# Scan stage of a one-layer backbone: round order of a pass, and 256 KB transfers issued one after another

## The chip, the cores and the metric

The kernel runs on one core of one Trainium2 chip. The metric is device time in microseconds of one execution; lower is better.

## The reference

One layer on 2048 latent and 256 context tokens of width 1024: modulated norm, an input projection, two mixers, a merge, and an expert-choice mixture of experts. The scan stage computes the recurrent cores of both mixers. For RWKV-7, in two directions and 8 heads of 64:

```python
def rwkv7_scan(inputs, s0):
    def step(s, inp):
        r_t, w_t, k_t, v_t, kk_t, a_t = inp
        sa = jnp.einsum('bhvk,bhk->bhv', s, -kk_t)
        s = (s * w_t[:, :, None, :] + sa[..., None] * (kk_t * a_t)[:, :, None, :]
             + v_t[..., None] * k_t[:, :, None, :])
        return s, jnp.einsum('bhvk,bhk->bhv', s, r_t)
```

and for the RG-LRU a causal convolution of 4 taps, two gates, `bt = sqrt(-expm1(2 log_a)) * (ig * xc)`, and the scan `h = a h + bt` over time, 512 channels, two directions.

## The kernel before, in words

The program is a sequence of stages written with explicit semaphores; each engine's order is the order of the code, so an instruction that waits holds up everything behind it on its engine. `scan` (L2111) is one of the stages. It makes 18 passes (`LAST` is 17), each over 256 tokens of a direction pair, cut into four chunks of 64. `U` counts two units of four heads.

A call `body(a, c)` interleaves two passes: `a` is solved (the triangular system of each chunk), while `c`, the pass before, is carried through its four chunks of state. The solve of `a` has five rounds (`begin`, `joint`), the **begin phase**, and then five doubling levels:

- round 0: L and its transpose Lt from `aq` and `ob`, 64x64 matmuls into banks 2 and 3 of each unit; ACT copies L, DVE masks Lt into T (T0);
- rounds 1 and 2 (`joint`): products B and K of both units side by side, `ob` with `aq` and `over` with `over`, 64x128 matmuls. Unit 0 does B first and unit 1 K first. DVE evicts each with eight masked multiplies (W0 and Lb from B, La and Lk from K);
- round 3: transposes tB and V; round 4: the transpose tK; ACT copies all three;
- level m: F = H x W (`forward`), ACT copies F; W and T products (`square`), DVE adds them to W and T. POOL makes the masked H of each level from L, and adds the unit matrix to T0 and W0 (`start_solve`).

Between the rounds and levels, at the places of the table `STATE_AT` (X, Z, S with Y for chunks 0 to 3), PE does the state products of pass `c`, and ACT, DVE and POOL the steps of the RG-LRU: at X the gates (ACT) and the series (DVE), at Z the roots and squares (ACT, with two table loads in chunk 0) and the taps (DVE), at S the window (ACT) and, in chunks 0 and 2, two recurrences (DVE). Every engine follows this same order.

Operands come from HBM. `ob` and `over` have one buffer a unit and `aq` has two, since the states read it a pass later. SP waits for tK of both units and then issues the next pass's `ob` and `over` (`reload`, L2225 to L2227); after Y3 and Sb3 of both units come `aq` of the pass after next (`reload_own`, L2223) and eight stores of y (`store`, L2246). It waits for no landing. POOL meanwhile sums `w_mod` slices of 512 KB each (`load`, `add`, L2752 to L2764), ACT loads the convolution's rows `raw` of 1 MB (`load_raw`, L2460). Helper lines: L2273 is every 64x64 matmul of the solve, L2288 every joint one, L2607 every eviction of B and K.

## Time and profile before

| | |
|---|---|
| median of 3 runs | 4309.09 us (4306.44 to 4311.71) |
| the profiled execution | 4309.31 us, its span 4307.5 us |
| mean granted clock of TensorE | 0.932 of full speed |
| PE busy | 3596.5 us, 83% of the span |
| DVE, ACT, POOL busy | 2432.9, 1889.2, 1258.8 us |
| moved by DMA | 610.18 MB, mean 142 GB/s |

How to read it: busy times overlap across engines, and a busy share of a whole span is an average over stages with different limits. Times in rows are microseconds from the first instruction. A clock of 1.00 is 2.4 GHz, 0.50 is 1.2 GHz. A wait put down to "issue" is one for which the profile shows no semaphore's release just before.

### The profile page before, as it was taken

To read this page: it belongs to the slowest core of one execution; us is meant where nothing else is said; L and a number is where in the kernel's file an instruction comes from. 1 tells how busy PE (TensorE), PEld (TensorE's weight loads), DVE (VectorE), ACT (ScalarE), POOL (GpSimd) and SP (SyncE) were. 2 spreads that over 40 slices of the span, in tenths; PEclk is the share of its full clock that TensorE was granted. 3 is DMA by queue.
4 is the path that set the end of the run, shared out by engine and by line. 5 is a ranking of instruction groups with operands and counts; after the bars stand their busy time and mean duration, and the time that the engine had idled before them with its cause. 6 is when DMAs were issued, how large, how long until landed. Compare 5 with 4: busy or idle time off the path is not lost. (4 is left out here: it accounts for less than half of the span.)

```text
span 4307.5 us, 117683 instructions
## 1 busy us (share of the span) xinstructions
PE 3596.5 (83%) x50061; PEld 3199.9 (74%) x50061; DVE 2432.9 (56%) x4389; ACT 1889.2 (44%) x3285; POOL 1258.8 (29%) x1250
## 2 busy tenths in 40 slices
PE   5799999999677777877777588894599999999992
PEld 2678888888577676777667488672499999999992
DVE  3237676510156666677767654435666666666664
ACT  3246665521154555555555443331244444444444
POOL 2223333311254655555553254000001010101110
PEclk8899999999898999999999799996699999999996
DMA  5235555532433333332331574431367676767675
GB/s 173 69 127 180 170 185 168 171 111 71 117 72 83 93 82 83 83 92 79 87 96 35 175 229 142 147 127 40 115 196 221 195 219 198 214 203 209 208 207 196
DMA packets 566343, 610.18 MB, mean 142 GB/s; under 512 B 65938, under 2 KB 471252, under 8 KB 564820
## 3 DMA queue, kind: packets, MB, share of 16 engines
q1 hardware_dynamic: 515540, 487.01, 36.9%
q0 software_dynamic: 21536, 76.56, 6.2%
q10 hardware_dynamic: 28768, 39.16, 2.8%
q8 instruction: 411, 6.73, 0.6%
q14 instruction: 88, 0.72, 0.1%
HBM read 443.09 MB, written 159.40 MB: 140 GB/s over the span
## 5 line engine op out<-in xcount | busy, mean ns | idle before, releaser
L339 DVE TENSOR_TENSOR moe_w_lo<-moe_w_lo_whole,moe_w_hi 128x2048 fp32r<-128x2048 f32 (+1 forms) x258 | 453.6, 1758 | 263.5 <-ACT moe_w_hi L517 188.0
L460 PE MATMUL moe_h<-moe_xt_hi,moe_w_hi 128*128 128x256 f32 x2048 | 582.0, 284 | 15.9 <-DVE moe_xt_lo L339 14.8
L460 PE MATMUL moe_h<-moe_xt_lo,moe_w_hi 128*128 128x256 f32 x2048 | 580.1, 283 | 0.6 <-issue 0.6
L460 PE MATMUL moe_h<-moe_xt_hi,moe_w_lo 128*128 128x256 f32 x2048 | 580.1, 283 | 0.0
L1792 PE MATMUL inward_pp<-u_u_hi,inward_w_hi 128*128 128x512 f32 (+1 forms) x1360 | 527.4, 388 | 20.8 <-POOL inward_w_lo L1952 20.8
L1792 PE MATMUL inward_pp<-u_u_lo,inward_w_hi 128*128 128x512 f32 (+1 forms) x1360 | 515.7, 379 | 0.0
L1792 PE MATMUL inward_pp<-u_u_hi,inward_w_lo 128*128 128x512 f32 (+1 forms) x1360 | 515.5, 379 | 0.0
L460 PEld LDWEIGHTS moe_h<-moe_xt_hi,moe_w_hi 128*128 128x128 f32 x2048 | 393.2, 192 | 27.9 <-issue 23.7
L460 PEld LDWEIGHTS moe_h<-moe_xt_lo,moe_w_hi 128*128 128x128 f32 x2048 | 393.3, 192 | 3.7
L460 PEld LDWEIGHTS moe_h<-moe_xt_hi,moe_w_lo 128*128 128x128 f32 x2048 | 393.3, 192 | 1.1 <-issue 0.8
L412 POOL DMA_INDIRECT scratch_x<-moe_ys,moe_who x32 | 70.6, 2205 | 912.2 <-DVE moe_ys L568 907.4
L1792 PEld LDWEIGHTS inward_pp<-u_u_hi,inward_w_hi 128*128 128x128 f32 x1360 | 257.1, 189 | 80.1 <-POOL inward_w_lo L1952 21.0
L1792 PEld LDWEIGHTS inward_pp<-u_u_hi,inward_w_lo 128*128 128x128 f32 x1360 | 257.0, 189 | 48.8
L1792 PEld LDWEIGHTS inward_pp<-u_u_lo,inward_w_hi 128*128 128x128 f32 x1360 | 257.4, 189 | 46.3
L2273 PE MATMUL scan_b<-scan_F,scan_T 64*64 64x64 f32 x5760 | 218.2, 228 | 61.4 <-issue 55.2
L2273 PE MATMUL scan_b<-scan_W,scan_H 64*64 64x64 f32 x5760 | 212.6, 227 | 52.0 <-issue 35.1
L1916 ACT ACTIVATE inward_out<-inward_pp 128x512 f32<-128x512 f32 (+1 forms) x170 | 97.6, 577 | 354.7 <-PE inward_pp L1792 353.7
L2273 PEld LDWEIGHTS scan_b<-scan_F,scan_T 64*64 64x64 f32 x5760 | 196.5, 141 | 76.2 <-issue 68.4
L503 ACT ACTIVATE moe_w_hi<-moe_w_lo_whole 128x2048 fp32r<-128x2048 f32 x128 | 243.4, 1901 | 0.1
L2273 PEld LDWEIGHTS scan_b<-scan_W,scan_H 64*64 64x64 f32 x5760 | 193.9, 141 | 65.0 <-issue 64.2
L2784 POOL TENSOR_TENSOR scan_H<-scan_L,scan_masks 128x512 f32<-128x512 f32 x180 | 237.9, 1351 | 4.5 <-PE scan_b L2273 4.5
L517 ACT ACTIVATE moe_w_hi<-moe_w_lo_whole 128x1024 fp32r<-128x1024 f32 x128 | 135.6, 1060 | 223.8 <-PE moe_y L443 223.8
(374 smaller groups left out, 9832.1 us busy)
## 6 DMA issues: line engine op xcount, KB each, us to landing
moe_w_lo_whole<-in_moe_w SPq DMA_DIRECT2D x387, 512.0 KB, 5.0
scratch_ops<-inward_ops SPq DMA_DIRECT2D x72, 514.0 KB, 3.8
scan_over<-scratch_ops SPq DMA_DIRECT2D x72, 512.0 KB, 9.9
inward_w_lo_whole<-in_w_in SPq DMA_DIRECT2D x38, 512.0 KB, 4.6
scan_aq<-scratch_ops SPq DMA_DIRECT2D x36, 516.0 KB, 5.0
scratch_gates<-inward_out SPq DMA_DIRECT2D x64, 256.0 KB, 2.2
all_late<-in_w_mod POOLq DMA_DIRECT2D x32, 512.0 KB, 4.5
rest_modsum<-scratch_gates SPq DMA_DIRECT2D x64, 256.0 KB, 4.4
```

The lines of the kernel that those rows point to most:

```text
L339: return nc.vector.tensor_tensor(x_lo, x, x_hi.bitcast(F32), ALU.subtract)
L412: pool.indirect_dma_start(env["x1"], bass.IndirectOffsetOnAxis(who[u][h][:, :], 0), ys[:, u, h, :], None, compute_op=ALU.add).then_inc(s_s ...
L460: mm = nc.tensor.matmul(hb[ft % 2][m][:, 0:CAP], w_, x, start=(k == 0 and part == 0), stop=(k == KD - 1 and part == 2))
L503: AC.did(f"{u}w13h{ft}", act.activation(w13_hi[:, to], w13[:, at], ACT.Copy))
L517: AC.did(f"{u}w2h{ft}", act.activation(w2_hi[:, to], w2[:, at], ACT.Copy))
L1792: mm = nc.tensor.matmul(pp[k % NB][:, 0:size], wx, ux, start=(kk_ == 0 and part == 0), stop=(kk_ == KD - 1 and part == 2))
L1916: act.activation(out[:, k % R, 0:size], pp[k % NB][:, 0:size], func).then_inc(s_ev, 1)
L2273: mm = nc.tensor.matmul(bank[u][to][other if across else h, k * HD:(k + 1) * HD], lhs(h, k), rhs(h, k), start=True, stop=True)
L2784: PO[u].did(f"H{m}", pool.tensor_tensor(four(H[u][(m - 1) % 3][:, :, :]), four(L[u][:, :, :]), masked(f"lev{m}t"), ALU.mult))
```

## The change

The rounds of the begin phase come in another order: tB and V in round 0, tK in round 1, L and Lt in round 2, the joint products in rounds 3 and 4. Round 0 now waits for `ob` and `over`, round 2 for `aq` and for tK's copy, and F1 for the last eviction of the second joint product. The places of `STATE_AT` stay. On POOL the first square step of pass `c` and the first level's H go ahead of the additions of the unit.

SP issues `ob` and `over` after the second joint product, as ten pieces of 256 KB, each issued when the one before has landed. `aq` comes in four pieces of 264 KB, in turns with the y stores, each awaited too; at a pass's end SP waits for the y stores. The first pass's loads are not awaited. POOL loads `w_mod` in two halves with a semaphore each, the next half when one is used up. ACT loads `raw` in four parts, two of them a step later. No arithmetic changes.

```diff
-        PE = [Steps(n.sem(f"pe_solve{u}"), ["L", "Lt"] + list(FIRST_OF[u]) + ["tB", "V", "tK"] + level_pe) for u in U]
-        AC = steps("act_solve", ["L", "tB", "V", "tK"] + [f"F{m}" for m in LEVELS])
+        PE = [Steps(n.sem(f"pe_solve{u}"), ["tB", "V", "tK", "L", "Lt"] + list(FIRST_OF[u]) + level_pe) for u in U]
+        AC = steps("act_solve", ["tB", "V", "tK", "L"] + [f"F{m}" for m in LEVELS])
         DV = [Steps(n.sem(f"dve_solve{u}"), ["T0"] + [f"{x}{d}" for p in FIRST_OF[u] for x in EVICTED[p] for d in U] +
                     [f"{x}{m}" for m in LEVELS for x in "TW" if m < 5 or x == "W"]) for u in U]
-        PO = steps("pool_solve", ["T0", "W0"] + [f"H{m}" for m in LEVELS])
+        PO = steps("pool_solve", ["H1", "T0", "W0"] + [f"H{m}" for m in LEVELS[1:]])
...
+            def own(it, u, d):
+                sp.dma_start(aq[u][:, it % 2, d, :], env["ops"][:, it][u][:, d, 2 * G:4 * G + 4]).then_inc(s_aq[u][it % 2], 16)
+
+            def own_landed(it, u, d):
+                sp.wait_ge(s_aq[u][it % 2], 32 * (it // 2) + 16 * d + 16)
+
+            def load(it, wait):
                 src = env["ops"][:, it]
                 for u in U:
-                    if own:
-                        sp.dma_start(aq[u][:, it % 2, :, :], src[u][:, :, 2 * G:4 * G + 4]).then_inc(s_aq[u][it % 2], 16)
-                    if rest:
-                        sp.dma_start(ob[u][:, :, :], src[u][:, :, 4 * G + 4:OPS]).then_inc(s_ob[u], 16)
-                        sp.dma_start(over[u][0:HD, :, :], src[u][HD:P, :, 0:4 * G]).then_inc(s_over0[u], 16)
-                        sp.dma_start(over[u][HD:P, :, :], src[u][0:HD, :, 0:4 * G]).then_inc(s_over1[u], 16)
+                    sp.dma_start(ob[u][:, :, :], src[u][:, :, 4 * G + 4:OPS]).then_inc(s_ob[u], 16)
+                    if wait:
+                        sp.wait_ge(s_ob[u], 16 * it + 16)
+                for d in range(2):
+                    for u in U:
+                        sp.dma_start(over[u][0:HD, d, :], src[u][HD:P, d, 0:4 * G]).then_inc(s_over0[u], 16)
+                        if wait:
+                            sp.wait_ge(s_over0[u], 32 * it + 16 * d + 16)
+                        sp.dma_start(over[u][HD:P, d, :], src[u][0:HD, d, 0:4 * G]).then_inc(s_over1[u], 16)
+                        if wait:
+                            sp.wait_ge(s_over1[u], 32 * it + 16 * d + 16)
 
             def reload(it):
+                PE[0].wait(sp, "K", it)
+                PE[1].wait(sp, "B", it)
+                load(it + 1, True)
+
+            def store(it, u):
+                ACc[u].wait(sp, "Y3", it)
...
+            def pass_end(it):
                 for u in U:
-                    PE[u].wait(sp, "tK", it)
-                load(it + 1, False, True)
-
-            def reload_own(it):
+                    if it + 2 <= LAST:
+                        PEc[u].wait(sp, "Y3", it)
+                        DVc[u].wait(sp, "Sb3", it)
+                        own(it + 2, u, 0)
+                        own_landed(it + 2, u, 0)
+                    store(it, u)
+                    if it + 2 <= LAST:
+                        own(it + 2, u, 1)
+                        own_landed(it + 2, u, 1)
                 for u in U:
-                    PEc[u].wait(sp, "Y3", it)
-                    DVc[u].wait(sp, "Sb3", it)
-                load(it + 2, True, False)
-
-            def store(it):
...
+                    sp.wait_ge(s_y[u], 64 * (it + 2))
 
             n_main = sum(k for _, k in CONST_SIZES)
-            load(0, True, True)
+            load(0, False)
+            for u in U:
+                for d in range(2):
+                    own(0, u, d)
             sp.dma_start(masks[:, :], t["consts"][:, n_main:n_main + len(MASKS) * P]).then_inc(s_masks, 16)
-            load(1, True, False)
+            for u in U:
+                for d in range(2):
+                    own(1, u, d)
             reload(0)
             for it in range(LAST + 1):
                 if it + 2 <= LAST:
                     reload(it + 1)
-                    reload_own(it)
-                store(it)
-            for u in U:
-                sp.wait_ge(s_y[u], 64 * (LAST + 2))
+                pass_end(it)
...
             def joint(r, a):
                 it, b, half = a
-                uB, uK = (0, 1) if r == 1 else (1, 0)
+                uB, uK = (0, 1) if r == 3 else (1, 0)
                 for u in U:
-                    if r == 1:
+                    if r == 3:
                         AC[u].wait(pe, "L", it)
                         DV[u].wait(pe, "T0", it)
                     else:
                         DV[u].wait(pe, EVICTED[FIRST_OF[u][0]][1] + "1", it)
-                pe.wait_ge(s_over0[uK], 16 * it + 16)
-                pe.wait_ge(s_over1[uK], 16 * it + 16)
...
                 oA, oB = of_ops(aq[u], b, 0), of_ops(ob[u], None, 0)
                 xV, xK = (of_ops(over[u], None, k * G) for k in range(2))
                 if r == 0:
-                    pe.wait_ge(s_aq[u][b], half * 16 + 16)
                     pe.wait_ge(s_ob[u], 16 * it + 16)
+                    pe.wait_ge(s_over0[u], 32 * it + 32)
+                    pe.wait_ge(s_over1[u], 32 * it + 32)
                     DV[u].wait(pe, "W5", it - 1)
-                    two(u, ("L", 2, oA, oB), ("Lt", 3, oA, oB))
-                elif r == 3:
-                    DV[u].wait(pe, second_done[u], it)
                     two(u, ("tB", 2, oB, unit), ("V", 3, xV, unit))
-                else:
+                elif r == 1:
                     AC[u].wait(pe, "tB", it)
                     for k in range(8):
                         mm = one(u, 2, xK, unit, True, k)
                     PE[u].did("tK", mm)
+                else:
+                    pe.wait_ge(s_aq[u][b], half * 32 + 32)
+                    AC[u].wait(pe, "tK", it)
+                    two(u, ("L", 2, oA, oB), ("Lt", 3, oA, oB))
 
             def forward(u, m, a):
...
                     DV[u].wait(pe, f"W{m - 1}", it)
                 else:
                     PO[u].wait(pe, "W0", it)
-                    AC[u].wait(pe, "V", it)
+                    DV[u].wait(pe, second_done[u], it)
...
-                    if a is not None and r in (1, 2):
+                    if a is not None and r in (3, 4):
...
                 it, b, _ = a
-                if r == 0:
+                if r == 2:
                     PE[u].wait(act, "L", it)
                     PO[u].wait(act, "H5", it - 1)
                     AC[u].did("L", act.activation(flat(L[u][:, :, :]), bank[u][2][:, :], ACT.Copy))
-                elif r == 3:
+                elif r == 0:
                     PE[u].wait(act, "tB", it)
                     AC[u].did("tB", act.activation(flat(tB[u][b][:, :, :]), bank[u][2][:, :], ACT.Copy, scale=-1.0))
                     PE[u].wait(act, "V", it)
                     AC[u].did("V", act.activation(flat(V[u][b][:, :, :]), bank[u][3][:, :], ACT.Copy))
-                elif r == 4:
+                elif r == 1:
                     PE[u].wait(act, "tK", it)
                     AC[u].did("tK", act.activation(flat(tK[u][b][:, :, :]), bank[u][2][:, :], ACT.Copy))
...
-                    act.dma_start(raw[:, CTX:], src[:, LAT0:LAT0 + SEQ]).then_inc(s_lat, 16)
+                    n_ = SEQ // 4
+                    act.dma_start(raw[:, CTX + part * n_:CTX + (part + 1) * n_], src[:, LAT0 + part * n_:LAT0 + (part + 1) * n_]).then_inc(s_lat, 16)
...
-                if r == 0:
+                if r == 2:
                     PE[u].wait(dve, "Lt", it)
                     D.did("T0", dve.tensor_tensor(four(T[u][:, :, :]), banked(bank[u][3]), masked("lev0t"), ALU.mult))
-                elif r in (1, 2):
-                    product = FIRST_OF[u][r - 1]
+                elif r in (3, 4):
+                    product = FIRST_OF[u][r - 3]
                     PE[u].wait(dve, product, it)
...
-            def load(part_):
+            def load(part_, x):
                 if part_ < 4 * KD:
-                    at, half = part_ // 2, part_ % 2
-                    pool.dma_start(wm, w_mod[:, NJ * half:NJ * (half + 1), 2 * D + at * G:2 * D + (at + 1) * G]).then_inc(s_wm, 16)
+                    at, k = part_ // 2, NJ * (part_ % 2) + NJ // 2 * x
+                    pool.dma_start(wm[:, NJ // 2 * x:NJ // 2 * (x + 1), :], w_mod[:, k:k + NJ // 2, 2 * D + at * G:2 * D + (at + 1) * G]).then_inc(s_wm[x], 16)
 
             def add(part_, count):
                 at, half = part_ // 2, part_ % 2
                 dst = env["modsum"][:, at * G:(at + 1) * G]
-                pool.wait_ge(s_wm, 16 * (part_ + 1))
                 for k in range(NJ):
+                    if k % (NJ // 2) == 0:
+                        pool.wait_ge(s_wm[k // (NJ // 2)], 16 * (part_ + 1))
...
-                load(part_ + 1)
+                    if k % (NJ // 2) == NJ // 2 - 1:
+                        load(part_ + 1, k // (NJ // 2))
                 return count
 
             def start_solve(it):
+                level(1, it)
                 for u in U:
                     for name, x in (("T0", T[u]), ("W0", W[u])):
                         DV[u].wait(pool, name if name == "T0" else "W01", it)
...
             for it in range(LAST + 2):
                 more, first = it <= LAST, 4 * (it - 1)
+                squares(first)
                 if more:
                     start_solve(it)
-                squares(first)
                 if more:
-                    level(1, it)
                     level(2, it)
```

ACT, from the copies of round 0 of a middle pass on, before:

```order
L2430 ACTIVATE scan_L<-scan_b 128x512 x2
L2448 ACTIVATE scan_X<-scan_b 128x128
L2450 ACTIVATE scan_Sd<-scan_S,scan_aq 128x64 x2
L2448 ACTIVATE scan_X<-scan_b 128x128
L2450 ACTIVATE scan_Sd<-scan_S,scan_aq 128x64 x2
L2511 ACTIVATE all_late<-scan_b,scan_lc 128x256
L2514 ACTIVATE scan_gated<-scan_b,scan_lc 128x256
L2535 ACT_TABLE_LOAD
L2535 ACTIVATE scan_root<-scan_root 128x1024
L2525 ACT_TABLE_LOAD
```

and the stretch that ends with the copies of L, as changed:

```order
L2539 ACTIVATE scan_gated<-scan_b,scan_lc 128x256
L2458 ACTIVATE scan_tK<-scan_b 128x512 x2
L2560 ACT_TABLE_LOAD
L2560 ACTIVATE scan_root<-scan_root 128x1024
L2550 ACT_TABLE_LOAD
L2550 ACTIVATE scan_decay<-all_late,scan_lc 128x256
L2552 ACTIVATE all_late<-scan_decay 128x256
L2553 ACTIVATE all_late<-all_late,scan_lc 128x256
L2554 ACTIVATE scan_root<-all_late,scan_lc 128x256
L2450 ACTIVATE scan_L<-scan_b 128x512 x2
```

The copies of L, for which the first joint product waits, moved from ahead of the gates, table loads and squares to behind them.

DVE, from the evictions of the first joint product on, before:

```order
L2607 TENSOR_TENSOR scan_Lk<-scan_b,scan_masks 128x256 x2
L2633 COPY scan_Z<-scan_b 128x128 x2
L2652 SCALAR_TENSOR_TENSOR all_late<-scan_win,all_cols,all_late 128x256 x3
L2658 SCALAR_TENSOR_TENSOR scan_gated<-scan_gated,all_late 128x256
L2607 TENSOR_TENSOR scan_La<-scan_b,scan_masks 128x256 x2
L2607 TENSOR_TENSOR scan_Lk<-scan_b,scan_masks 128x256 x2
L2607 TENSOR_TENSOR scan_W<-scan_b,scan_masks 128x256 x2
L2607 TENSOR_TENSOR scan_Lb<-scan_b,scan_masks 128x256 x2
L2638 SCALAR_TENSOR_TENSOR scan_S<-scan_b,scan_aq,scan_Sd 128x64 x4
L2674 SCALAR_TENSOR_TENSOR scan_root<-scan_gated,scan_root 128x256
```

and, as changed, from the second recurrence of chunk 0 to the evictions of the second product:

```order
L2700 SCALAR_TENSOR_TENSOR scan_root<-scan_gated,scan_root 128x256
L2707 SCALAR_TENSOR_TENSOR scan_root<-scan_decay,scan_root 128x256
L2717 COPY all_late<-scan_root 128x8x32
L2633 TENSOR_TENSOR scan_W<-scan_b,scan_masks 128x256 x2
L2633 TENSOR_TENSOR scan_Lb<-scan_b,scan_masks 128x256 x2
L2633 TENSOR_TENSOR scan_La<-scan_b,scan_masks 128x256 x2
L2633 TENSOR_TENSOR scan_Lk<-scan_b,scan_masks 128x256 x2
L2689 TENSOR_TENSOR scan_root<-scan_root,all_late 128x256
L2691 SCALAR_TENSOR_TENSOR scan_root<-scan_root,all_late 128x256
L2694 COPY_PREDICATED scan_root<-scan_large,all_late 128x256
L2633 TENSOR_TENSOR scan_La<-scan_b,scan_masks 128x256 x2
L2633 TENSOR_TENSOR scan_Lk<-scan_b,scan_masks 128x256 x2
```

Both joint evictions now stand behind the recurrences of chunk 0, where before both stood ahead of them.

## Rows read from the trace of the kernel before

**Rows 1.** The page: busy time, and the queue that carries instructions.

```profile
PE 3596.5 (83%) x50061; PEld 3199.9 (74%) x50061; DVE 2432.9 (56%) x4389; ACT 1889.2 (44%) x3285; POOL 1258.8 (29%) x1250
...
q8 instruction: 411, 6.73, 0.6%
```

**Rows 2.** Windows: length, busy us of PE, PEld, DVE, ACT, POOL; clock, DMA share, GB/s.

```profile
1684.30:1710.50 26.20, 19.16 (x708) 17.73 (x705) 22.41 (x43) 16.23 (x37) 19.53 (x19) 1.00 0.21 56
1710.50:1755.80 45.30, 35.14 (x1184) 33.65 (x1185) 24.81 (x57) 20.89 (x53) 20.48 (x23) 0.85 0.37 91
1192.60:2299.00 1106.40, 840.30 (x30211) 797.43 (x30209) 749.21 (x1578) 587.53 (x1427) 597.43 (x608) 0.93 0.33 85
```

**Rows 3.** Waits of PE, 1192.6 to 2299: total us, times, longest.

```profile
PE scan_b L2273 <- issue: 134.8, 91, 7.0
PE scan_b L2288 <- issue: 38.4, 16, 2.4
PE scan_b L2383 <- DVE scan_Z L2633: 29.3, 14, 3.3
```

**Rows 4.** Windows, columns as in rows 2: single blocks of 256 instructions of PE.

```profile
2063.73:2067.64 3.91, 3.06 (x129) 2.78 (x127) 2.40 (x8) 3.88 (x11) 0.00 (x0) 1.00 0.02 4
2050.55:2059.16 8.61, 3.14 (x134) 3.01 (x132) 2.16 (x8) 3.96 (x11) 6.35 (x6) 0.98 1.03 219
1721.82:1727.78 5.96, 5.96 (x125) 5.68 (x127) 0.29 (x1) 3.18 (x10) 0.00 (x0) 0.50 0.01 3
1746.09:1752.23 6.14, 3.29 (x127) 2.94 (x128) 2.48 (x4) 0.83 (x2) 1.73 (x3) 0.96 1.03 307
1821.49:1824.95 3.46, 3.26 (x126) 3.07 (x127) 1.37 (x2) 0.60 (x1) 1.55 (x2) 1.00 0.43 112
```

**Rows 5.** Timeline of PE at the end of pass 8's longest stall.

```profile
1721.82 0.26 PE L2368 MATMUL scan_b<-scan_V,scan_La 64*64 64x64 f32 x1 [4.90 <-issue]
```

**Rows 6.** DMA issues, 1192.6 to 2299: count, KB each, median us to landing.

```profile
scan_over<-scratch_ops SPq DMA_DIRECT2D x64, 512.0 KB, 9.8
scan_aq<-scratch_ops SPq DMA_DIRECT2D x32, 516.0 KB, 5.0
...
scan_ob<-scratch_ops SPq DMA_DIRECT2D x32, 256.0 KB, 6.6
scratch_y<-scan_y SPq DMA_DIRECT2D x128, 64.0 KB, 3.8
```

**Rows 7.** DMA issues, 1705.8 to 1706.45: one load of ob into quiet.

```profile
scan_ob<-scratch_ops SPq DMA_DIRECT2D x1, 256.0 KB, 3.4
```

**Rows 8.** Timeline of SP's issues at the end of pass 8.

```profile
1746.12 5.86 SPq L2246 DMA_DIRECT2D scratch_y<-scan_y  x8
```

**Rows 9.** Groups on PE, 1694.3 to 1710.6: busy us, mean ns, idle before.

```profile
L2273 PE MATMUL scan_b<-all_consts,scan_ob 64*64 64x64 f32 x64 | 2.3, 221 | 1.2 <-DVE scan_Lk L2607 1.0 <-DVE scan_Lb L2607 0.2
...
L2288 PE MATMUL scan_b<-scan_aq,scan_ob 64*64 64x128 f32 x32 | 2.0, 271 | 2.4 <-issue 2.4
```

**Rows 10.** Timeline of ACT, pass 8: first table load and last square step.

```profile
1691.32 1.28 ACT L2535 ACT_TABLE_LOAD   x1
...
1696.43 0.58 ACT L2529 ACTIVATE scan_root<-all_late,scan_lc 128x256 f32<-128x256 f32 x1
```

**Rows 11.** Timeline of DVE, pass 8: evictions of a product, recurrences of chunk 0.

```profile
1691.57 0.76 DVE L2607 TENSOR_TENSOR scan_W<-scan_b,scan_masks 128x256 f32<-128x256 f32 x2 [1.99 <-PE scan_b L2288]
...
1693.57 0.75 DVE L2607 TENSOR_TENSOR scan_Lk<-scan_b,scan_masks 128x256 f32<-128x256 f32 x2
...
1701.85 0.42 DVE L2674 SCALAR_TENSOR_TENSOR scan_root<-scan_gated,scan_root 128x256 f32<-128x256 f32 x1
...
1706.74 1.27 DVE L2691 COPY all_late<-scan_root 128x256 f32<-128x256 f32 x1
```

**Rows 12.** Timeline of POOL, pass 8: the unit added to W0.

```profile
1700.58 1.28 POOL L2774 TENSOR_TENSOR scan_W<-scan_W,all_consts 128x512 f32<-128x512 f32 x1 [3.74 <-DVE scan_W L2607]
```

**Rows 13.** Waits of PE in the first pass, 1118 to 1160.

```profile
PE scan_b L2288 <- DVE scan_T L2599: 5.7, 1, 5.7
```

More of the change, by code:

```diff
@@ L2178, in scan @@
         s_masks, s_sum, s_zero = n.sem("masks_loaded"), n.sem("mod_summed"), n.sem("state_zero")
-        s_wm = n.sem("wm_loaded")
+        s_wm = [n.sem(f"wm_loaded{x}") for x in range(2)]
         block = ctx.enter_context(nc.Block())
@@ L2218, in _ @@
         def _(sp):
-            def load(it, own, rest):
+            def own(it, u, d):
[3 more added lines that the diff above has]
+            def load(it, wait):
                 src = env["ops"][:, it]
                 for u in U:
-                    if own:
-                        sp.dma_start(aq[u][:, it % 2, :, :], src[u][:, :, 2 * G:4 * G + 4]).then_inc(s_aq[u][it % 2], 16)
-                    if rest:
-                        sp.dma_start(ob[u][:, :, :], src[u][:, :, 4 * G + 4:OPS]).then_inc(s_ob[u], 16)
-                        sp.dma_start(over[u][0:HD, :, :], src[u][HD:P, :, 0:4 * G]).then_inc(s_over0[u], 16)
-                        sp.dma_start(over[u][HD:P, :, :], src[u][0:HD, :, 0:4 * G]).then_inc(s_over1[u], 16)
@@ L2229, in reload @@
-            def reload(it):
-                for u in U:
-                    PE[u].wait(sp, "tK", it)
-                load(it + 1, False, True)
-            def reload_own(it):
-                for u in U:
-                    PEc[u].wait(sp, "Y3", it)
-                    DVc[u].wait(sp, "Sb3", it)
-                load(it + 2, True, False)
-            def store(it):
-                for u in U:
-                    ACc[u].wait(sp, "Y3", it)
-                    for d in range(2):
-                        for h in range(2):
-                            dst = env["y"][d, bass.ds(it, 1), :, u * P + h * HD:u * P + (h + 1) * HD].rearrange("o (c s) v -> s (o c) v", s=HD)
-                            sp.dma_start(dst, y[u][64 * h:64 * h + 64, 4 * d:4 * d + 4, :]).then_inc(s_y[u], 16)
+                    sp.dma_start(ob[u][:, :, :], src[u][:, :, 4 * G + 4:OPS]).then_inc(s_ob[u], 16)
@@ new lines, in reload @@
+            def reload(it):
+                PE[0].wait(sp, "K", it)
[4 more added lines that the diff above has]
+                for d in range(2):
+                    for h in range(2):
+                        dst = env["y"][d, bass.ds(it, 1), :, u * P + h * HD:u * P + (h + 1) * HD].rearrange("o (c s) v -> s (o c) v", s=HD)
+                        sp.dma_start(dst, y[u][64 * h:64 * h + 64, 4 * d:4 * d + 4, :]).then_inc(s_y[u], 16)
@@ L2248, in _ @@
             n_main = sum(k for _, k in CONST_SIZES)
-            load(0, True, True)
+            load(0, False)
+            for u in U:
+                for d in range(2):
+                    own(0, u, d)
             sp.dma_start(masks[:, :], t["consts"][:, n_main:n_main + len(MASKS) * P]).then_inc(s_masks, 16)
-            load(1, True, False)
+            for u in U:
+                for d in range(2):
+                    own(1, u, d)
             reload(0)
@@ L2255, in _ @@
                     reload(it + 1)
-                    reload_own(it)
-                store(it)
-            for u in U:
-                sp.wait_ge(s_y[u], 64 * (LAST + 2))
+                pass_end(it)
         @block.tensor
@@ L2476, in window @@
                 else:
-                    act.wait_ge(s_lat, 16 * (j + 1))
+                    act.wait_ge(s_lat, 64 * (j + 1))
                 if k:
@@ L2502, in window @@
                 elif k % (2 * NG) == 2 * NG - 1 and j + 1 < NJ:
-                    load_raw(j + 1, "latents")
+                    for part_ in range(2):
+                        load_raw(j + 1, part_)
+                elif k % (2 * NG) == 0 and k:
+                    for part_ in range(2, 4):
+                        load_raw(j, part_)
             def gates(k):
@@ L2583, in _ @@
             load_raw(0, "context")
-            load_raw(0, "latents")
+            for part_ in range(4):
+                load_raw(0, part_)
             act.wait_ge(s_zero, 3)
@@ L2798, in _ @@
             pool.wait_ge(s_masks, 16)
-            load(0)
+            for x in range(2):
+                load(0, x)
             count = 0
```

## The prediction, made before the changed kernel ran

> **What bounds the kernel now.** I read the page first, then the time by stage, then the waits of PE, then short stretches around them. PE is busy for 83% of the span [rows 1], and the change touches only the scan, so its passes are what matters. Eighteen passes lie between 1124 and 2391 us; the sixteen from 1192.6 to 2299 take 1106.4 us, 69.15 each, with PE busy in 840.3 of them at a mean clock of 0.93 [rows 2]. A pass has a begin phase (five rounds, until chunk 1's state update follows level product F1) and a level phase. Pass 8 shows them: 26.2 us with PE busy for 19.2, then 45.3 with PE busy for 35.1, to the start of pass 9 [rows 2]. That pass is 2.3 us longer than the mean; with its begin phase taken as typical, the level phase averages 43 us.
>
> Among PE's waits the largest are not for any engine: 134.8 us before the matmuls of L2273 are put down to "issue", the largest for an engine, for DVE's Z, is 29.3 us [rows 3]. "Issue" means two things here. The 38.4 us before L2288 are 16 waits of at most 2.4 us, equal from pass to pass: the second joint product waits for DVE to evict the first. The others come at a fixed count. Between the ends of two such stalls PE starts 129 matmuls and 127 weight loads, 256 in all, in 3.91 us [rows 4]; the page has 411 instruction packets of 16.4 KB on average, and PE's 100,122 instructions over 256 make 391 of them [rows 1]. So PE runs through blocks of 256 instructions and stalls where the next has not arrived. This block ran under 4 GB/s of other traffic, with matmuls in 3.06 of its 3.91 us: even in quiet PE in the levels is near the rate of its instruction fetch. Where six loads (2.5 MB) were issued at once, a block took 8.61 us under 219 GB/s; the last block of a pass, under two operand loads and the first stores, 6.14 us under 307 GB/s [rows 4]. The longest stall of pass 8 is 4.90 us [rows 5]; the block behind it ran at a granted clock of 0.50 (1.2 GHz) and took 5.96 us [rows 4].
>
> **Change, part by part: the transfers.** Per pass SP issues two 256 KB loads of ob and four 512 KB loads of over without a wait, landing after a median of 6.6 and 9.8 us [rows 6]; now ten pieces of 256 KB, one at a time. An ob load issued into quiet lands after 3.4 us [rows 7], so ten take about 34 us, a rate of 77 GB/s. A block under 112 GB/s of y stores took 3.46 us [rows 4]: nothing measurable. The bounds for a piece in flight are thus 0 (that row) and the full excess of a burst, 8.61 - 3.8 = 4.8 us over one block. I take 0.2 us for each of the nine blocks in those 34 us, near the moderate row: 1.8 us. What it removes: one long stall a pass; the longest of all is 7.0 [rows 3], and I take pass 8's 4.9 for the mean, 0.7 of it ordinary, so 4.2. Then the half clock behind it: a mean of 0.93 puts 14% of a pass, 9.7 us, at 1.2 GHz, and I count three quarters of one such block to the long stall, 0.75 x (5.96 - 3.8) = 1.6. Of the 2.3 us excess of the last block 1.7. That is 7.5 removed, 1.8 added, and another 1.0 for blocks under the smaller pieces of operands, y and w_mod, which now overlap for longer: **4.7 us gained in the level phase**. The raw row and w_mod pieces move the same bytes; POOL's four issues a pass in place of two cost it about 1.6 us of a queue that idles anyway.
>
> A rule of the skill speaks against small pieces. The page "DMA: Bandwidth & Descriptors", section Bandwidth, advises batching transfers to 1 MiB or more for three quarters of the peak rate. By it ten serial pieces are slow, which is true and harmless as long as they are done in time; the sum would change only if they were not.
>
> Are they in time? The loads start when the second joint product is done, about 23 us into a pass, and round 0 of the next pass wants ob and over: some 44 us against 34. Ten microseconds of slack cover pieces of up to 4.4 us. The aq operands are tighter. They start after Y3 of unit 0, about 9 us before the pass ends; four pieces of 3.4 us and the eight y issues between them (5.86 us [rows 8]) end about 19.5 us later, 10 us into the next pass. L of unit 1 wants the last at about 8. PE then waits some 1.5 us, but ACT is not ready before 12.8 (below), so I cost it at 0.4. The later round of L is what makes this possible.
>
> **The order of the begin phase.** Work is the same on every engine; the dependences are not. Timetable from the start of a pass: tB and V of both units take 2.3 us of PE [rows 9]; X0 until 4.2; ACT evicts four tiles, two X, and runs the gates until about 5.9, then tK until 7.0. Next in ACT's queue now stand the root's table load, the roots, the second table load and the squares, 5.7 us (1691.32 to 1697.01 [rows 10]), and only then L: both copies are out at 13.9. Before, L was evicted ahead of all this. The first joint product starts at 14.0, after an idle of 1 to 2 us, and ends at 16.0 (2.0 us [rows 9]); X1 follows until 17.8.
>
> DVE has S0's update done at about 12.5. Next in its queue stand the two recurrences, which stood behind both joint evictions before: from 1701.85 to 1708.01 they took 6.2 us [rows 11]. I take 5.9, until 18.4 (bounds 4 and 8: both were seen to stretch while POOL works). Then the eight evictions of the first product, 2.75 us (1691.57 to 1694.32 [rows 11]), until 21.2: the second product waits 3.5 us where it waited 2.4. It takes 2.0 us, more at the half clock that such an idle may bring (I add 1.1), and ends at 24.4. Its evictions follow at once; unit 1's W0 is out after six of eight, at 26.5, and POOL's addition of the unit takes 1.28 [rows 12], so F1 of unit 1 runs until 29. The next state update, which before waited 29.3/16 = 1.8 us for Z [rows 3], then waits for nothing. Begin phase 29.5 against 26.2: **3.3 us lost**. Bounds: 27.0 if the recurrences find POOL idle and the clock stays at 2.4 GHz, 32 if the operands land 3 us later.
>
> POOL's own reordering costs nothing: H1 and T0 fit between 13.4 and 21 and H2 is wanted only after two more PE steps. SP's extra waits have behind them only its own next pieces and y stores, and y is not rewritten before the next pass's first Y.
>
> **Sum.** A pass changes by 3.3 - 4.7 = -1.4 us; seventeen of either make -24. In the first pass the joint product waited 5.7 us for T0 and so for the masks [rows 13] with three rounds still to come; two of the three are now done in that time: -6. Together -30. The profiled execution took 4309.31 us around its span of 4307.5, and the median of the runs is 4309.09, so one base serves: 4309 - 30 = **4279 us**.
>
> **Rivals.** (1) *Operands late, slower.* If pieces land after 4.7 us under the y stores (a y store's own landing takes 3.8, aq's median is 5.0 [rows 6]), four pieces and the issues take 25 us and end 15.5 us into the pass. L of unit 1 then starts there; S0, the recurrences under POOL's work, both products and F1 follow, and the begin phase takes about 32.3: 6.1 lost against 4.7 gained, 17 x 1.4 - 6 = +18, 4327. It decides from about 4.2 us a piece. For it: several landings in the rows are long. Against it: those had megabytes queued ahead.
> (2) *Fetch fully relieved, faster.* PE in the levels goes by blocks of 3.8 us without further excess and the begin phase loses only 1.5: 17 x (1.5 - 6.0) - 6 = -82, 4227. For it is the row at 112 GB/s; against it DVE's queue.
> (3) *The stalls are no fetch.* Then smaller pieces change nothing and only the begin phase counts: 17 x 3.3 - 6 = +50, 4359. The count of 256 speaks against it. The page "Runtime: NRT & Kernel Launch", section Instruction fetch mechanics, says that engines take instructions in 16 KiB blocks of 256, fetched ahead and mostly hidden. By that rule this rival would hold; the rows agree with the block and not with the hiding.
> (4) *Both cancel*: about 4309.
>
> **How the numbers follow.** Forecast 0.50, with a range of its own from 4250 to 4305; operands late 0.20; fully relieved 0.17; no fetch 0.05; cancelled 0.08. The predicted time is the likeliest, 4279. The range takes in rivals 1 and 2 and stops short of 3: 4225 to 4335. A measurement of this kernel can tell about 0.2% (9 us) from no change. Faster by more has most of the forecast and rival 2: 0.64; within 0.2% has rival 4 and the forecast's edge: 0.12; slower has rivals 1 and 3 and the edge: 0.24.
>
> **What would show it.** Right: in the levels no block over 5 us and no stall over 2 us at "issue"; ob and over pieces landing 3.2 to 3.8 us after issue; ACT's L after the squares; the second joint product waiting near 3.5 us for DVE, with the begin phase near 29 us and the level phase near 38; a mean clock above 0.93. Wrong: PE waiting for aq before L or for over in round 0 by more than 1 us a pass; blocks under a single piece at 5 us or more; or a begin phase above 31 us.

## The result, and the profile after

The changed kernel takes 4340.58 us (median of 7 runs, 4323.51 to 4344.08) against 4307.6 for the kernel before (7 runs beside it, 4304.7 to 4311.71): a ratio of 1.0071, with a 95% interval of 1.0058 to 1.0084. It is slower by 0.7%, where 0.7% faster was forecast, and outside the range.

The page's busy times, which answer to [rows 1]:

```profile
PE 3611.4 (83%) x50061; PEld 3211.4 (74%) x50061; DVE 2419.2 (56%) x4389; ACT 1894.4 (44%) x3285; POOL 1261.4 (29%) x1282
...
q8 instruction: 411, 6.73, 0.7%
```

Windows of the changed kernel, as [rows 2]: pass 8's begin phase, its level phase, and the sixteen passes.

```profile
1675.10:1708.10 33.00, 20.68 (x702) 19.19 (x703) 19.39 (x45) 18.47 (x41) 13.75 (x14) 0.90 0.27 65
1708.10:1745.30 37.20, 30.40 (x1200) 28.76 (x1195) 27.07 (x55) 18.50 (x48) 24.53 (x27) 1.00 0.36 92
...
1197.80:2314.10 1116.30, 842.75 (x30209) 796.20 (x30211) 737.39 (x1580) 592.83 (x1429) 606.71 (x635) 0.93 0.33 84
```

The granted clock stayed at 0.93. From now on begin and level phases are means over the sixteen passes 1 to 16, taken from the starts of round 0 and of chunk 1's state update in PE's rows. Before they were 26.1 and 43.1 us; now they are 32.9 and 37.0. Both terms of the forecast are there, but the begin phase has lost 6.8 us and the levels have gained 6.0. The passes together cost 10 us more.

PE's waits in the same stretch, as [rows 3]:

```profile
PE scan_b L2293 <- issue: 85.8, 93, 2.8
PE scan_b L2293 <- DMA scan_aq<-scratch_ops: 72.0, 15, 8.9
PE scan_b L2308 <- DVE scan_Lk L2633: 29.9, 16, 3.6
PE scan_b L2293 <- DVE scan_Lk L2633: 17.9, 16, 1.3
```

The fetch stalls (waits at "issue" at the end of a block of PE's code) fell from 134.8 to 85.8 us and the longest from 7.0 to 2.8 (2 was forecast at most). In their place stands a wait that was not there: 72.0 us for aq, ahead of L, almost once a pass. Two of the prediction's signs of being wrong are met: 72.0/16 = 4.5 us a pass for aq, where 1 was the limit, and a begin phase above 31 us.

The larger part of the loss is not in the scan. By the last rows of each stage, the changed kernel is 8 us behind when the choice of experts ends (3061.4 before, 3069.7 now) and 34 us when the mixture of experts ends (4231.4 and 4265.3). No line of that stage was changed. Its eight repeats of PE's loop, windows of the kernel before and then of the changed one:

```profile
3085.00:4232.00 1147.00, 1128.04 (x7936) 1054.24 (x7936) 724.76 (x865) 485.38 (x494) 136.03 (x90) 1.00 0.66 201
```

```profile
3093.00:4266.00 1173.00, 1136.47 (x7936) 1062.66 (x7936) 724.22 (x865) 486.14 (x494) 127.84 (x90) 0.99 0.65 196
```

The loop takes 26 us more for the same 7936 matmuls. PE's waits at "issue" in these windows, in the kernel before and in the changed one:

```profile
PE moe_h L460 <- issue: 0.6, 1, 0.6
```

```profile
PE moe_h L460 <- issue: 17.8, 7, 3.2
```

The end of the first of these seven stalls in the changed kernel's timeline of PE:

```profile
3243.24 0.39 PE L460 MATMUL moe_h<-moe_xt_hi,moe_w_lo 128*128 128x256 f32 x1 [3.24 <-issue]
```

Windows of the changed kernel, the 22 us before that point (with the stall) and the 4 us behind it:

```profile
3222.00:3244.00 22.00, 17.98 (x119) 15.97 (x119) 17.14 (x24) 10.82 (x12) 1.68 (x1) 1.00 0.60 189
3243.20:3247.20 4.00, 3.96 (x22) 3.96 (x23) 0.48 (x1) 0.00 (x0) 3.56 (x2) 0.62 1.03 268
```

The stall stands before the same matmul, the 18th of the loop, in the second to the eighth repeat, those that the loop's branch leads into; the first repeat has none. Before the stall shown the granted clock was 1.00, and in the 4 us behind it 0.62 on average. Windows of 4 us behind the others have 0.57 to 0.69, but 1.00 behind the shortest, of 1.54 us. So 17.8 us of stalls and 8.4 us more of busy PE make the 26.

### The profile page after: what moved, and what is told of

It is laid out like the page before. It is cut to its first block and busy times, and to the rows that moved or that the text cites. A ratio compares the mean times of both kernels' runs of the same rounds, so it can differ in the third digit from the quotient of the medians.

```text
span 4338.8 us, 117920 instructions
## 1 busy us (share of the span) xinstructions
PE 3611.4 (83%) x50061; PEld 3211.4 (74%) x50061; DVE 2419.2 (56%) x4389; ACT 1894.4 (44%) x3285; POOL 1261.4 (29%) x1282
## 5 line engine op out<-in xcount | busy, mean ns | idle before, releaser
L460 PE MATMUL moe_h<-moe_xt_hi,moe_w_lo 128*128 128x256 f32 x2048 | 585.2, 286 | 17.8 <-issue 17.8
L2293 PE MATMUL scan_b<-scan_F,scan_T 64*64 64x64 f32 x5760 | 209.3, 224 | 22.7 <-issue 16.9
```

Source lines behind the costliest of these rows:

```text
L460: mm = nc.tensor.matmul(hb[ft % 2][m][:, 0:CAP], w_, x, start=(k == 0 and part == 0), stop=(k == KD - 1 and part == 2))
L2293: mm = nc.tensor.matmul(bank[u][to][other if across else h, k * HD:(k + 1) * HD], lhs(h, k), rhs(h, k), start=True, stop=True)
```

## The theories

The changed scan has 35 more separate waits on PE, counted in the built program: 850 instead of 815. So PE's code behind it lies 35 instructions further. I call this its layout: where the head of the later loop, its first instruction, lies in a block of 256. If each matmul counts as a weight load and a matmul, twice over for float32, and each such wait as one, then all 24 stalls at issue of over 1.5 us in the changed scan end on one place, two counts wide, modulo 256, and so do 38 of the 39 of the scan before that are not the second joint product's waits. The seven stalls of the loop lie 10 counts off that place; instructions in between that no row shows may account for it, which is not shown. The loop's stall is 38 instructions behind its head (17 matmuls, each with its weight load, and four more); in the kernel before the same place was 73 behind it. Its trace agrees: its one stall at issue in the loop, short as it is, stands before the 35th matmul of a repeat, 17 matmuls or 34 instructions further on.

```profile
3377.06 0.28 PE L460 MATMUL moe_h<-moe_xt_lo,moe_w_hi 128*128 128x256 f32 x1 [0.56 <-issue]
```

**Theory A** has three parts: this distance costs the stalls in the mixture of experts; the serial loads of ob and over do what was forecast in the levels; and the late aq takes it back. The rivals stand in the expectations.

## The experiments

A pad is a row of instructions that only move the code behind them; here they are increments of a semaphore that nobody reads. Ratios are to the kernel before, on the same chip, with 95% intervals.

**e1: the kernel before, with the changed kernel's layout**

```diff
+            for _ in range(35):
+                n.apart(pe)
             PE.start(pe)
             pe.wait_ge(s_g[0], 32)
```

> The kernel before, with 35 semaphore increments that nobody reads, on PE ahead of the mixture of experts' first step. The changed scan has 35 more waits on PE, so from here on PE's code lies as in the changed kernel: the loop's head 38 instructions before the end of a block of 256 instead of 73. Theory A (layout): the stage takes 1196 us instead of 1170, PE stalls at issue once in each repeat, 1.5 to 3.3 us, before the 18th matmul of the loop, and the time is 4330 to 4336 us (ratio 1.005 to 1.0065). Rival B (the stage is slower for what the scan leaves behind, or from execution to execution): 4302 to 4312 us, no such stalls.

4330.05 us, ratio 1.0049 (1.0034 to 1.0064). Window over its loop, with the columns of [rows 2]:

```profile
3091.00:4257.00 1166.00, 1132.98 (x7936) 1058.91 (x7936) 724.89 (x866) 486.46 (x494) 126.12 (x91) 0.99 0.65 197
```

and PE's waits at issue in it:

```profile
PE moe_h L462 <- issue: 13.7, 7, 2.4
```

The seven stalls came, before the 18th matmul again, with nothing changed in the scan. Rival B is out. About 6 us of the slowdown are the pad itself, ahead of the loop; the repeats took 1159 us against 1142 before and 1167 changed, since the stalls were shorter here.

**e2: the changed kernel, with the layout of before**

```diff
+            for _ in range(221):
+                n.apart(pe)
             PE.start(pe)
```

> The changed kernel, with 221 such increments ahead of the mixture of experts, where PE waits 12 us for a gather: the loop's head lies again 73 instructions before the end of a block. Theory A (layout): the stage is back at 1170 us without the seven stalls, 4312 to 4318 us (ratio 1.001 to 1.0025). Rival B: 4336 to 4345 us, as the changed kernel.

4346.62 us, ratio 1.009 (1.0075 to 1.0104): by the time alone theory A would have fallen. The trace says otherwise. The stalls before the 18th matmul were gone (three of 0.5 to 0.7 us were left, before the 35th) and the repeats took 1142.5 us, but the loop began 58 us behind the last row of the stage before instead of 24: an increment took some 0.15 us of PE, and the weight loads wait for `PE.start` behind all 221. The run measured my pad; e5 has it in a place where it is hidden.

**e5: the changed kernel, padded behind `PE.start`**

```diff
             PE.start(pe)
+            for _ in range(44):
+                n.apart(pe)
             pe.wait_ge(s_g[0], 32)
```

> The changed kernel with 44 unread increments on PE, now behind the step that frees the weight loads and ahead of the 12 us wait for the gather, so that their 6 to 7 us are hidden. The loop's head lies 250 instructions before the end of its block. Theory A (layout: only the distance from the head to the end of its block counts, and 38 is too short): the seven stalls go, the eight repeats take 1142 us and not 1167, and the time is 4312 to 4318 us (ratio 1.001 to 1.0025). Rival B (what counts is another place in the loop, such as the branch at its end): the repeats stay above 1155 us, 4330 us or more.

4317.91 us, just inside theory A's 4312 to 4318; the ratio, 1.0029 (1.0018 to 1.004), is a little above its 1.0025. The loop is as before to the microsecond, and no wait at issue is listed in it:

```profile
3081.00:4228.00 1147.00, 1128.02 (x7936) 1054.27 (x7936) 727.33 (x866) 485.38 (x494) 136.20 (x90) 1.00 0.67 201
```

So the layout costs 0.42% or **18 us**, more than half of the slowdown, with the two intervals leaving some 7 us either way. In the traces the repeats took 1167.1 us in the changed kernel and 1141.4 here, 26 us less. Distances of 73 and of 250 serve equally. A pad moves every place of the loop together, so its times alone don't say which place counts; that it is the block's end behind the head is read from where the stalls stand, 38 and about 73 instructions in. The later experiments on the changed order carry this pad too.

**e3: serial loads of ob and over alone, in the old order**

```diff
+                        if it:
+                            sp.wait_ge(s_ob[u], 16 * it + 16)
+                for d in range(2 if rest else 0):
+                    for u in U:
+                        sp.dma_start(over[u][0:HD, d, :], src[u][HD:P, d, 0:4 * G]).then_inc(s_over0[u], 16)
+                        if it:
+                            sp.wait_ge(s_over0[u], 32 * it + 16 * d + 16)
...
```

> The kernel before, with its order of rounds and its operands aq as they were; only ob and over come as ten pieces of 256 KB, each issued when the last has landed. Theory A (the level phase's 6 us came from the serial loads; the begin phase's loss from the new order and the late aq): the level phase is 37 to 38 us instead of 43, the begin phase stays at 26 to 26.5, 4308 - 16 x 5.5 = 4220 us (4210 to 4235). Rival B (the gain came with the order of the rounds, the loads matter little): level phase 42 to 43 us, 4295 to 4310 us. Rival C (the ten pieces end too late for round 0 here): PE waits for over in round 1 of the next pass, over 4250 us.

4246.35 us, ratio 0.985 (0.9833 to 0.9867): **1.5% faster than before**. That is 65 us (60 by the medians), if less than theory A's 4210 to 4235. Begin phase 26.4 us, level phase 39.0. PE's waits in passes 1 to 16:

```profile
PE scan_b L2281 <- issue: 87.7, 87, 3.3
PE scan_b L2296 <- issue: 39.0, 17, 2.4
PE scan_b L2391 <- DVE scan_Z L2641: 28.7, 15, 3.3
PE scan_b L2281 <- DMA scan_aq<-scratch_ops: 19.8, 11, 5.4
```

The fetch stalls fell as in the changed kernel (134.8 to 87.7), and rivals B and C are out: PE waited for over once, 2.2 us. The levels gained 4.1 us and not 5.5. Of the difference 19.8/16 = 1.2 us a pass is aq, unchanged here, which now comes late at times.

**e4 and e7: aq issued at once, ahead of the stores, in the new order**

```diff
-                        own_landed(it + 2, u, 0)
-                    store(it, u)
-                    if it + 2 <= LAST:
                         own(it + 2, u, 1)
-                        own_landed(it + 2, u, 1)
+                for u in U:
+                    store(it, u)
```

> The changed kernel with the layout of e2, and the four pieces of aq issued without waits between them and ahead of the y stores. Theory A (aq late costs its whole wait): the 74.7 us before L go, some 1.5 us a pass come back as a fetch stall under the burst at the pass's end, 4315 - 75 + 24 = 4264 us (4255 to 4275). Rival B (what stands behind aq, ACT's squares ahead of L's copy and DVE's recurrences ahead of the evictions, ends last anyway): PE then waits there instead, 20 to 30 us gained, 4285 to 4295 us.

> e4 with the increments of e5 in place of the 221, which held the weight loads back by 34 us. Theory A: 4290 - 34 = 4256 us (4250 to 4262), against 4315 for e5: the waits for aq cost 55 to 60 us. Rival B (the 34 us at the stage's head were not on the path): 4280 to 4290 us.

e4, with the 221 increments: 4290 us, 0.9967 (0.9953 to 0.9981). By the time alone that is rival B's 4285 to 4295 and not theory A's 4255 to 4275. But both were reckoned from 4315, without the 34 us of the pad, and e2, which has the pad, took 4346.62: against it e4 gains 1.23% or 53 us. e7: 4262.49 us, 0.9891 (0.9877 to 0.9906), so the 34 us of the pad were on the path, as theory A had it. Against e5 that is 1.4% or **59 us** (55 by the medians), and PE waits for aq no more. A part of rival B is true as well: PE now waits more for ACT's copy of L, in e7

```profile
PE scan_b L2308 <- ACT scan_L L2450: 18.6, 15, 2.8
```

against 3.8 us in the changed kernel. The begin phase fell from 31.8 us in e5 to 28.8; the level phase is 38.3 against 37.2, for which the burst at the pass's end is the likely reason (e10, without the burst, has 37.4). The passes of these two traces differ by 1.8 us only, those of e2 and e4 by 3.6: the profiled execution of e5 was its fastest, 4303 us, and that of e7 its slowest, 4278.

**e10: aq awaited piece by piece, but ahead of the stores**

```diff
-                        own(it + 2, u, 0)
-                        own_landed(it + 2, u, 0)
-                    store(it, u)
-                    if it + 2 <= LAST:
-                        own(it + 2, u, 1)
-                        own_landed(it + 2, u, 1)
+                        for d in range(2):
+                            own(it + 2, u, d)
+                            own_landed(it + 2, u, d)
+                for u in U:
+                    store(it, u)
```

> e5 with the four pieces of aq still awaited one by one, but all four ahead of the y stores. They start as in the changed kernel about 5.5 us before the pass ends and take 4 x 3.5 = 14 us, so the last lands about 8.5 us into the pass instead of 15, where PE wants it at 8. Theory A (the y stores in between are what makes aq late): PE's waits for aq fall from 70 to 15 us or less, 4318 - 50 = 4268 us (4260 to 4278). Rival B (waiting for each piece is enough to be late, since the ten pieces before end too late): 35 us of waits stay, 4285 to 4300 us.

4263.65 us, 0.9905 (0.9886 to 0.9925), not to be told from e7. PE's waits in the sixteen passes, where 7.0 us are left of e5's 64.8 for aq:

```profile
PE scan_b L2294 <- issue: 94.1, 98, 3.3
PE scan_b L2309 <- DVE scan_Lk L2634: 34.0, 16, 4.5
PE scan_b L2294 <- DVE scan_Lk L2634: 21.6, 16, 1.9
...
PE scan_b L2294 <- DMA scan_aq<-scratch_ops: 7.0, 3, 2.7
```

Awaiting each piece costs nothing that can be told here. The stores in between were what the pieces could not afford.

**e6: the new order alone**

```diff
-                load(it + 1, True)
+                load(it + 1, False)
```

(and the aq of e7)

> The changed order of rounds with ob and over not awaited (the ten pieces issued at once), aq issued ahead of the stores without waits, and the 44 increments of e5. Theory A (order alone loses the 2.2 us that e4's begin phase has over the one of before, and the level phase is back at 43 us): passes of 71 us, 4306 + 17 x 2.2 - 6 = 4337 us (4325 to 4345). Rival B (the late begin of the new order is itself worth something in the levels): level phase 40 us or less, under 4300 us.

4318.36 us, 1.0027 (1.0015 to 1.0039), below theory A's 4325 and above B's 4300. The fetch stalls are back:

```profile
PE scan_b L2293 <- issue: 134.9, 100, 5.6
PE scan_b L2308 <- DVE scan_Lk L2633: 27.3, 16, 4.6
```

The begin phase is 28.2 us, 2.2 above before, as expected; the level phase is 41.2, 1.8 below, which neither theory had. So all that e6 still has of the change, above all the new order, costs **12 us** (6 to 17 by its interval); the pieces themselves, POOL's new order and the cuts of w_mod and the rows are in it too, and only these last were run by themselves (e11). The serial loads give 59 us in the new order (e6 to e7, where the pieces are the same and only the waits come in) and 65 in the old (before to e3, pieces and waits together).

**e8: each unit's aq as soon as its own states are done**

```diff
                     PEc[u].wait(sp, "Y3", it)
                     DVc[u].wait(sp, "Sb3", it)
-                load(it + 2, True, False)
+                    sp.dma_start(aq[u][:, it % 2, :, :], env["ops"][:, it + 2][u][:, :, 2 * G:4 * G + 4]).then_inc(s_aq[u][it % 2], 16)
```

> e3 with the aq load of each unit issued as soon as this unit's Y3 and Sb3 are done, not after both. Theory A: of e3's 19.8 us of PE waiting for aq some 10 to 15 go, 4246 - 12 = 4234 us. Rival B (unit 1's load is the late one and starts no earlier): 4243 to 4249 us.

4250.17 us, 0.9874 (0.9858 to 0.9889): no gain over e3, and PE waited 30.3 us for aq in its sixteen passes. That is rival B: nothing is won for the unit that is late.

**e9: the serial loads in 512 KB pieces of over**

```diff
-                for d in range(2 if rest else 0):
-                    for u in U:
-                        sp.dma_start(over[u][0:HD, d, :], src[u][HD:P, d, 0:4 * G]).then_inc(s_over0[u], 16)
...
+                for u in U if rest else ():
+                    sp.dma_start(over[u][0:HD, :, :], src[u][HD:P, :, 0:4 * G]).then_inc(s_over0[u], 16)
...
```

> e3 with over in four pieces of 512 KB instead of eight of 256 KB, still each issued when the last has landed. Theory A (what relieves PE's instruction fetch is that one transfer is in flight at a time, not its size): level phase 38 to 40 us as in e3, 4240 to 4252 us. Rival B (a fetch waits for what is queued, and a piece of 512 KB is twice the queue): half of the gain goes, 4265 to 4285 us.

4277.25 us, 0.9931 (0.991 to 0.9952): half of e3's gain is lost, as rival B had it. Its fetch stalls, from PE's waits in the sixteen passes:

```profile
PE scan_b L2280 <- issue: 131.5, 106, 3.5
```

and the landing of its pieces of over, from the DMA issues (count, KB each, median us):

```profile
scan_over<-scratch_ops SPq DMA_DIRECT2D x64, 512.0 KB, 4.9
```

A piece of 512 KB lands after 4.9 us, a rate of 107 GB/s, one of 256 KB after 3.5, 75 GB/s. The stalls sum nearly to what they were before the change, but none is above 3.5 us where the longest was 7.0. My theory that only one transfer in flight matters was wrong: size matters as much. The level phase is 41.4 us, against 39.0 in e3.

**e11: e3 with the halves of w_mod and the quarters of the rows**

```diff
-                pool.wait_ge(s_wm, 16 * (part_ + 1))
                 for k in range(NJ):
+                    if k % (NJ // 2) == 0:
+                        pool.wait_ge(s_wm[k // (NJ // 2)], 16 * (part_ + 1))
...
```

> e3 with the change's other two cuts: w_mod in two halves a step and the convolution's rows in four parts. Theory A (they overlap ob and over for longer and move the same bytes): nothing that can be measured, 4241 to 4252 us. Rival B (the long stalls left in e3 are under the 512 KB and 1 MB loads): another 1 us a pass, 4225 to 4235 us.

4242.38 us, 0.9845 (0.9824 to 0.9866). Not to be told from e3's 0.985; these two cuts do nothing measurable. e3 and e11 are the best versions found, 1.5% ahead of the kernel before and 2.2% ahead of the changed one.

## Why the prediction was wrong, step by step

The runs split the slowdown. From before to the changed kernel: the order +12 us (e6), the serial loads of ob and over -59 (e6 to e7), the aq pieces between stores +59 (e7 to e5), the layout +18 (e5 to the changed kernel). That is +30, and 4307 us times the ratio's 0.0071 is 31 (the medians differ by 33). The four add up because each run in the chain starts where the last one ended, so the sum is no check; each step is uncertain by 5 to 8 us. The traces split it 8 us in the scan and 26 in the mixture of experts.

**"4.7 us gained in the level phase"** was right in mechanism. In 17 passes it promised 80 us; the runs gave 59 to 65, and level phases shorter by 4.1 us (before to e3) and 2.9 (e6 to e7). The removed stalls and the half clock behind them were read from pass 8, whose level phase of 45.3 us was itself 2.2 above the mean. The landing of a piece was right: the medians of the changed kernel from 1197 to 2300 us, which answer to [rows 6]:

```profile
scan_over<-scratch_ops SPq DMA_DIRECT2D x128, 256.0 KB, 3.6
scan_aq<-scratch_ops SPq DMA_DIRECT2D x61, 258.0 KB, 3.4
...
scan_ob<-scratch_ops SPq DMA_DIRECT2D x32, 256.0 KB, 3.1
scratch_y<-scan_y SPq DMA_DIRECT2D x120, 64.0 KB, 2.6
```

**The rule on batching.** The Trainium skill, "DMA: Bandwidth & Descriptors", section Bandwidth, advises transfers of 1 MiB or more. For the transfer's own rate the runs agree (107 against 75 GB/s); for the time they don't: e9's larger pieces cost 31 us over e3, and PE's fetch stalls are 131.5 us with them against 87.7.

**"I cost it at 0.4"**, the wait for aq, is the step that failed: e5 to e7, e5 to e10 and e2 to e4 put it at 59, 53 and 53 us, 3.1 to 3.5 a pass. Rival 1 named the mechanism, but gave it to slow pieces, from 4.2 us on, and they took 3.4. SP's issues at the turn from pass 12 to 13, and behind them unit 1's L on PE, both from the timeline of the changed kernel, show what it was:

```profile
2010.15 0.44 SPq L2236 DMA_DIRECT2D scan_over<-scratch_ops  x1
2013.60 0.45 SPq L2233 DMA_DIRECT2D scan_over<-scratch_ops  x1
2017.28 0.45 SPq L2236 DMA_DIRECT2D scan_over<-scratch_ops  x1
2021.29 0.32 SPq L2220 DMA_DIRECT2D scan_aq<-scratch_ops  x1
2024.88 3.64 SPq L2250 DMA_DIRECT2D scratch_y<-scan_y  x4
2028.57 5.09 SPq L2220 DMA_DIRECT2D scan_aq<-scratch_ops  x2
2038.12 2.56 SPq L2250 DMA_DIRECT2D scratch_y<-scan_y  x4
2040.73 0.60 SPq L2220 DMA_DIRECT2D scan_aq<-scratch_ops  x1
...
2043.82 1.99 PE L2293 MATMUL scan_b<-scan_ob,scan_aq 64*64 64x64 f32 x64 [8.27 <-DMA scan_aq<-scratch_ops]
```

The first aq piece goes out at 2021.29, when the last piece of over has landed; Y3, for which I took SP to wait, was done by 2018.8. Pass 13 starts at 2026.3. In the mean of the sixteen passes the first aq piece is issued 5.6 us before a pass's end and the last 11.4 us into the next, 17 us later. The length of this chain I had (19.5 us with the landing); its start I had at 9 us before the end. It is late because the ten pieces are: they start 28.5 us into a pass in the mean, not 23, since the second joint product is late, and that product is late because L is, for want of aq. The one delay feeds the other (in e10, where L hardly waits, the ten start at 24.7), and my timetable of the begin phase was made once, without going round. The 10 us of slack that I found for ob and over were the same microseconds in which aq was to be issued; I counted them for one queue position and not for what stands behind it.

What I took to cover the wait holds in part. ACT's copies of L at the same turn:

```profile
2040.58 0.57 ACT L2450 ACTIVATE scan_L<-scan_b 128x512 f32<-128x512 f32 x1
2045.84 0.60 ACT L2450 ACTIVATE scan_L<-scan_b 128x512 f32<-128x512 f32 x1 [4.69 <-PE scan_b L2293]
```

ACT was through with the squares 14.3 us into the pass (12.8 was forecast), and still waited 4.69 us for the second unit's L.

**"3.3 us lost" in the order of rounds** was too much. e6 and e7 have 28.2 and 28.8 us for the begin phase, 2.2 to 2.7 above before. The second product waits 1.9 us for its eviction in the changed kernel (29.9/16), not 3.5: DVE was earlier than I timed it. The wait for Z is gone as forecast. Over the whole, the order costs 12 us and not the 17 x 2.9 - 6 = 43 that my sum holds for it without aq, for e6 also shows shorter levels. Why, is open; no run separates it.

**The first pass**, -6: pass 1 starts 5.4 us earlier (1187.2 against 1192.6), and the joint product's wait for T0 fell from 5.7 to 0.9 us. Right.

**The sum** counted the scan alone. "The change touches only the scan" was true of the lines and false of the program: 18 us came from where PE's code lies in a stage 700 us later. The rows of the two programs show no such thing, because waits that are instructions of their own have no row there. The Trainium skill states the rule that I had read past, in "Runtime: NRT & Kernel Launch", section Instruction fetch mechanics: a taken branch breaks the sequential fetch, and a target outside the window costs a fetch before work goes on. The trace agrees in that only the repeats entered by the branch stall. But the stall stands not at the target but 38 instructions behind it, at the next block; what the runs add is that the place of the head in its block decides (38 before its end: 1.5 to 3.2 us a repeat; 73: nothing or up to 0.9; 250: nothing).

The errors, in us, along the chain of runs above: aq 59 for the 7 of the sum (0.4 x 17), +52; the layout +18; the serial loads 59 for 80, +21; the order 12 for 43, -31. Together 60, where a change of -30 was forecast and +31 came. The prediction's timetable of the begin phase shows no place where its 0.4 enters, since it runs by DVE from 12.5 us on; if it is not in the 3.3, the first error is 59 and the last -38, and the sum is the same. That the errors in the scan partly cancel is luck: without the smaller loss by the order the kernel would have been 31 us slower still.

## What to carry to other kernels

A chain of awaited transfers on one queue has to be timed to its last member, and what comes behind it starts no earlier than its end: put the operand that the next step wants ahead of stores that nobody waits for. Where PE is near the rate of its own instruction fetch, small transfers one at a time are worth a few microseconds a pass, if nothing urgent stands behind them. And a change of a few instructions on PE ahead of a loop can cost more than the change itself; look at PE's waits at "issue" in the stages that were not touched, and compare the loop's first matmuls.

## What the runs showed of the hardware that I had not expected

- A loop on PE whose head lay 38 instructions before the end of a block of 256 stalled 1.5 to 3.2 us in every repeat that its branch led into, 17.8 us in all, and the granted clock fell from 1.00 to a mean of 0.62 in the 4 us behind the first of them. At 73 instructions stalls of at most 0.9 us were left, before the 35th matmul in place of the 18th; at 250 there was none.
- Fetch stalls of PE follow the size of the data transfers even when they come one at a time: 88 us of stalls under pieces of 256 KB (e3), 132 under 512 KB (e9).
- An increment of a semaphore took PE some 0.15 us: 221 of them put the loop back by 34 us, 35 of them by 5.7.
